# Seven modulation groups moved under the first feed forward, the scan's backward keys into the context attention

## The reference, cut to what matters

```python
s_lat = jax.nn.silu(c)[:, None, :]
s_ctx = jax.nn.silu(c_ctx)[None, None, :]
for i in range(DEPTH):
    need_ctx = i < DEPTH - 1
    ml = jnp.split(s_lat @ w_ada[i] + b_ada[i], 6, axis=-1)
    mc = jnp.split(s_ctx @ w_ada[i] + b_ada[i], 6, axis=-1)
    u_lat = modulate(h_lat, g_pre_mix[i], ml[0], ml[1])
    ...
    h_lat = h_lat + ml[2] * rms_norm_2(o_lat, g_post_mix[i])
    f_lat = sqrelu_mlp(modulate(h_lat, g_pre_ff[i], ml[3], ml[4]), w_ff1[i], w_ff2[i])
    h_lat = h_lat + ml[5] * rms_norm_2(f_lat, g_post_ff[i])
    if need_ctx:
        h_ctx = h_ctx + mc[2] * rms_norm_2(o_ctx, g_post_mix[i])
        ...
```

## Time and profile before

| | |
|---|---|
| median of 3 runs | 1934.95 us (1932.95 to 1937.16) |
| the profiled execution | 1936.78 us, span 1934.9 us |
| granted clock of PE, mean of the span | 0.995 |
| PE busy | 1869.8 us (97%) |
| DVE busy | 1105.8 us (57%) |
| ACT busy | 861.6 us (45%) |
| POOL busy | 211.9 us (11%) |

### The profile page before, as it was taken

The page is one execution under the profiler, slowest core; times in us unless marked ns, Lnnn a source line. Parts: engine busy times, 40 slices in busy tenths (PEclk is TensorE's granted clock), DMA queues, the critical chain, the costliest instruction groups (busy, mean ns, idle before and its releaser), DMA issues. The chain is left out here.

```text
span 1934.9 us, 37112 instructions
## 1 busy us (share of the span) xinstructions
PE 1869.8 (97%) x15824; PEld 1559.3 (81%) x15824; DVE 1105.8 (57%) x1835; ACT 861.6 (45%) x1559; POOL 211.9 (11%) x249
## 2 busy tenths in 40 slices
PE   7999999999999999999999999999999999899998
PEld 5768998776899788756898888888887798579986
DVE  6566774566667554476557665444444565546643
ACT  5465653446656542465322335322222254655532
POOL 2101221110122100103122211000000011000000
PEclk9999999999999999999999999999999999899999
DMA  7777665467766541353000042333332234024653
GB/s 267 250 256 224 189 183 175 166 227 263 223 166 195 175 142 55 115 174 110 26 4 4 4 151 65 104 119 98 100 107 88 66 99 139 25 88 133 194 180 124
DMA packets 219354, 264.68 MB, mean 137 GB/s; under 512 B 14214, under 2 KB 153782, under 8 KB 214711
## 3 DMA queue, kind: packets, MB, share of 16 engines
q1 hardware_dynamic: 218603, 261.49, 42.4%
q10 hardware_dynamic: 588, 0.82, 0.1%
HBM read 261.20 MB, written 1.09 MB: 136 GB/s over the span
## 5 line engine op out<-in xcount | busy, mean ns | idle before, releaser
L404 PE MATMUL acc<-rounded,rounded 128*128 128x512 f32 (+1 forms) x2552 | 875.1, 343 | 9.6 <-DVE rounded L684 4.1
L405 PE MATMUL acc<-rounded,rounded 128*128 128x512 f32 (+1 forms) x2552 | 867.0, 340 | 0.0
L406 PE MATMUL acc<-rounded,rounded 128*128 128x512 f32 (+1 forms) x2552 | 866.8, 340 | 0.0
L388 DVE TENSOR_TENSOR rounded<-arena,rounded 128x2048 fp32r<-128x2048 f32 (+1 forms) x194 | 434.3, 2241 | 285.9 <-ACT rounded L377 285.8
L404 PEld LDWEIGHTS acc<-rounded,rounded 128*128 128x128 f32 x2552 | 480.6, 188 | 80.1 <-issue 14.7
L405 PEld LDWEIGHTS acc<-rounded,rounded 128*128 128x128 f32 x2552 | 480.7, 188 | 60.0 <-issue 1.9
L406 PEld LDWEIGHTS acc<-rounded,rounded 128*128 128x128 f32 x2552 | 480.5, 188 | 60.0
L377 ACT ACTIVATE rounded<-arena 128x2048 fp32r<-128x2048 f32 (+1 forms) x194 | 362.9, 1873 | 341.6 <-PE acc L406 296.4
L1624 DVE SCALAR_TENSOR_TENSOR arena<-acc,pcol,arena 128x254 f32<-128x254 f32 (+1 forms) x176 | 76.8, 478 | 52.3 <-ACT arena L1605 50.8
L2200 PE MATMUL sc<-arena 64*64 64x64 f32 x2560 | 94.7, 221 | 8.8 <-DVE arena L2350 7.7
L2764 ACT ACTIVATE arena<-acc 128x512 f32<-128x512 f32 (+1 forms) x64 | 31.4, 490 | 159.6 <-PE acc L406 159.6
(11 more groups left out here) (265 smaller groups left out, 1691.6 us busy)
## 6 DMA issues: line engine op xcount, KB each, us to landing
arena<-in_w_ff SPq DMA_DIRECT2D x64, 1024.0 KB, 5.4
arena<-in_w_ada SPq DMA_DIRECT2D x48, 1024.0 KB, 5.1
arena<-in_w_up SPq DMA_DIRECT2D x88, 512.0 KB, 5.1
arena<-in_w_in SPq DMA_DIRECT2D x24, 1024.0 KB, 5.3
arena<-in_w_down SPq DMA_DIRECT2D x20, 1024.0 KB, 5.0
arena<-in_w_out SPq DMA_DIRECT2D x16, 1024.0 KB, 5.1
arena<-in_w_in_even SPq DMA_DIRECT2D x9, 1024.0 KB, 5.3
arena<-in_w_in_odd SPq DMA_DIRECT2D x8, 1024.0 KB, 5.2
```

Of the source, the lines that this page charges most:

```text
L388: dve.tensor_tensor(r32(w), w, r32(high_slot(c)[:, 0:size(c)]), ALU.subtract).then_inc(split_made, 1)
L404: pe.matmul(ps, ah, bh, start=first, stop=False)
L405: pe.matmul(ps, ah, bl, start=False, stop=False)
L406: return pe.matmul(ps, al, bh, start=False, stop=last)
```

## The change

- Blocks 16 to 22 leave attBl and attBc; only block 23 is still made in attBl's first two units, and attBc makes none. Each of the seven becomes two "late" chunks in the list, one ahead of ff1(e) and one ahead of the following ff2 (14 chunks). Their first half (4 of 8 row blocks) and second half are summed by DVE, four operations a chunk: 128 x 512 weights times the column of silu(c), into `late_sum`. PE then makes 4 products of `late_sum` with a matrix of ones (`late_pe`), which sum over the partitions and turn the row into columns, at the start of the second column block of ff2(e). DVE adds the bias. Only the latent stream's value is made.
- DVE makes the decays in projB, after the running sums; the keys of direction 0 in attBl's units 0 to 3, those of direction 1 in attBc's units 0 to 3.
- In all attentions by feature POOL copies the two reciprocals to 128 x 128 (`widen`), and PE transposes that in place of the two broadcast products. POOL's eight products of attBc are spread between these copies.
- Gains and gates of layer 1 are made in proj1 (one gain in scan step 0), its gates are transposed, stored and read back there.

The core of the diff (changed call arguments, buffers and bookkeeping of banks are left out):

```diff
@@ -326,6 +326,21 @@
                 partial[0] += 1
                 release.extend([(chunk_read, partial[0]), (sc_full, fill_of(n) + 1)])
 
+        late_read = sem("late_read")
+        late_chunk = []
+
+        def plan_late():
+
+            n = len(late_chunk)
+            view = I["w_ada_2"][1].rearrange("(k p) n -> p k n", p=P)
+            c, k0 = 512 * (4 + n // 2), 4 * (n % 2)
+            late_chunk.append(len(chunks))
+            whole.add(len(chunks))
+            chunks.append(view[:, k0:k0 + 4, c:c + 512])
+            release.append((late_read, n + 1))
+            if n % 2:
+                stage(("late", n // 2), tr=1)
+
         def is_up(g):
             return len(chunks[g].shape) == 4
 
...
@@ -383,6 +398,7 @@
             while splits["low"] < len(split_chunks) and split_chunks[splits["low"]] <= g:
                 n = splits["low"]
                 c = split_chunks[n]
+                late_dve(dve, c)
                 dve.wait_ge(high_made, n + 1)
                 w = raw_slot(c)[:, 0:size(c)]
                 dve.tensor_tensor(r32(w), w, r32(high_slot(c)[:, 0:size(c)]), ALU.subtract).then_inc(split_made, 1)
...
@@ -465,10 +481,9 @@
             stage(("prep", j), sc=2, tr=2)
         stage("kT", tr=4)
         stage("qT", tr=4)
-        stage("attBl", acc=16, tr=16 + 4, sc=8 + 4)
-        plan_ada(range(16, 20), lambda n: sc_at["attBl"] + 3 * n)
-        stage("attBc", acc=16, tr=8 + 4 + 8, sc=8 + 4)
-        plan_ada(range(20, 24), lambda n: sc_at["attBc"] + 3 * n)
+        stage("attBl", acc=16, tr=16 + 1, sc=8 + 1)
+        plan_ada([23], lambda n: sc_at["attBl"])
+        stage("attBc", acc=16, tr=8 + 8, sc=8)
         for s in range(NCH):
             if s == 1:
                 stage("gates", tr=1)
...
@@ -490,10 +505,14 @@
         EIGHTHS, ET = 8, FT2 // 8
 
         def plan_ff1(e):
+            if e:
+                plan_late()
             stage(("ff1", e), acc=ET)
             plan_feat(("ff1", e), I["w_ff1_2"][0][:, e * ET * P:(e + 1) * ET * P], pairs(ET * P), pair_fills(("ff1", e), ET))
 
         def plan_ff2(e):
+            if e < EIGHTHS - 1:
+                plan_late()
             stage(("ff2", e), acc=8)
             plan_tok(("ff2", e), I["w_ff2_2"][0][e * ET * P:(e + 1) * ET * P, :], ET, acc_at[("ff2", e)], [ALL] * 2)
             if e == EIGHTHS - 1:
...
@@ -898,17 +918,16 @@
                     for m in range(2):
                         pe.matmul(ps[m * HD:(m + 1) * HD, 0:P], self.v(u, m, kb), self.probT[:, u % 2, (m * n + kb) * P:(m * n + kb + 1) * P],
                                   start=(kb == 0), stop=(kb == n - 1), tile_position=(0, m * HD))
-                pe.wait_ge(att_comb, self.base + u + 1)
-                for m in range(2):
-                    ins = pe.matmul(ps[m * HD:(m + 1) * HD, P:2 * P], self.recip[:, 2 * u + m:2 * u + m + 1].broadcast_to([P, HD]), ident,
-                                    start=True, stop=True, tile_position=(0, m * HD))
+                i = self.featured.index(u)
+                pe.wait_ge(att_wide, self.spread_units + i + 1)
+                ins = pe.transpose(ps[:, P:2 * P], self.wide[:, i % 2, :], ident)
                 ins.then_inc(POOLS[self.values_at(u)[0]][1], 1)
 
             def tensor(self, pe, hook=None):
                 self.scores(pe, 0)
                 self.scores(pe, 1)
                 for u in range(self.n):
-                    if self.ada:
+                    if u < 2 * len(self.ada):
                         ada_pe(pe, self, u // 2, u % 2)
                     if self.group is not None and u % 2 == 0:
                         group_pe(pe, self.group, u // 2)
...
@@ -993,6 +1010,17 @@
                                             self.recip[:, 2 * u:2 * u + 2].unsqueeze(2).broadcast_to([P, 2, HD]), ALU.mult)
                 ins.then_inc(drain(*f), 1)
 
+            def widen(self, pool, before=None):
+
+                for i, u in enumerate(self.featured):
+                    if before and u in before:
+                        before[u]()
+                    pool.wait_ge(att_comb, self.base + u + 1)
+                    if i >= 2:
+                        pool.wait_ge(att_spread, self.spread_units + i - 1)
+                    pool.tensor_copy(self.wide[:, i % 2, :].rearrange("p (m e) -> p m e", m=2),
+                                     self.recip[:, 2 * u:2 * u + 2].unsqueeze(2).broadcast_to([P, 2, HD])).then_inc(att_wide, 1)
+
             def outputs_by_feature(self, dve, u):
 
                 f = self.values_at(u)
...
@@ -1238,7 +1266,46 @@
-        mod_gates = mod_gate.rearrange("p l w k s -> p (l w k s)")
+        gates_of = [mod_gate[:, l].rearrange("p w k s -> p (w k s)") for l in range(DEPTH)]
+        late_done = [0]
+
+        def late_dve(dve, c):
+
+            while late_done[0] < len(late_chunk) and late_chunk[late_done[0]] + 2 <= c:
+                n = late_done[0]
+                late_done[0] += 1
+                if n and n % 2 == 0:
+                    late_add(dve, n // 2 - 1)
+                g = late_chunk[n]
+                wait_landed(dve, g)
+                if n % 2:
+                    dve.wait_ge(late_read, n)
+                w = shaped(raw_slot(g), g)
+                for k in range(4):
+                    s = silu_c[:, 4 * (n % 2) + k, 0:1]
+                    if n % 2 == 0 and k == 0:
+                        ins = dve.tensor_scalar(late_sum, w[:, k, :], s, None, ALU.mult)
+                    else:
+                        ins = dve.scalar_tensor_tensor(late_sum, w[:, k, :], s, late_sum, ALU.mult, ALU.add)
+                    if k < 3:
+                        link(dve, ins)
+                ins.then_inc(late_read, 1)
+
+        def late_pe(pe, b):
+
+            pe.wait_ge(late_read, 2 * b + 2)
+            ps = claim(pe, "tr", tr_at[("late", b)])
+            for n in range(4):
+                ins = pe.matmul(ps[:, 2 * n:2 * n + 2], late_sum[:, n * P:(n + 1) * P], ones[:, 0:2], start=True, stop=True)
+            ins.then_inc(tr_full, 1)
+
+        def late_add(dve, b):
+
+            f = tr_at[("late", b)]
+            ps = filled(dve, "tr", f)
+            dve.tensor_tensor(mod[:, 1, 16 + 4 * b:20 + 4 * b, :], ps[:, 0:8].rearrange("p (a b) -> p a b", a=4),
+                              col("b_ada_2", 6 * KT + 16 + 4 * b, 4).unsqueeze(2).broadcast_to([P, 4, 2]), ALU.add)\
+               .then_inc(drain("tr", f), 1)
...
@@ -1328,18 +1395,32 @@
+        def pre_gain(dve, l, w):
+
+            scale = mod[:, l, (3 * w + 1) * KT:(3 * w + 2) * KT, :]
+            pre = col(("g_pre_mix_2", "g_pre_ff_2")[w], KT * l, KT).unsqueeze(2).broadcast_to([P, KT, 2])
+            return dve.scalar_tensor_tensor(mod_gain[:, l, w], scale, 1.0, pre, ALU.add, ALU.mult)
+
+        def post_gate(dve, l, w):
+
+            gate = mod[:, l, (3 * w + 2) * KT:(3 * w + 3) * KT, :]
+            post = col(("g_post_mix_2", "g_post_ff_2")[w], KT * l, KT).unsqueeze(2).broadcast_to([P, KT, 2])
+            return dve.tensor_tensor(mod_gate[:, l, w], gate, post, ALU.mult)
+
+        def ada_gains(dve):
+
+            wait_drained(dve, "tr", tr_at[("group_turn", 2)])
+            for w in range(2):
+                pre_gain(dve, 0, w)
+                post_gate(dve, 0, w).then_inc(mod_ready, 1)
+
+        def late_gains(dve):
+
+            wait_drained(dve, "tr", tr_at[("late", EIGHTHS - 2)])
+            wait_drained(dve, "tr", att_bl.ada_tr[0])
+            pre_gain(dve, 1, 1)
+            for w in range(2):
+                post_gate(dve, 1, w).then_inc(mod_ready, 1)
...
@@ -1505,6 +1586,9 @@
+
+        def pool_att1(pool, l):
+            att[("att1", l)].widen(pool, {13: lambda: subnorm_pool(pool, l)})
...
@@ -1730,6 +1816,7 @@
+        late_sum = Region(at_ff0_end + 9 * SEQ).take(512)
...
@@ -1913,6 +2000,8 @@
+            for d in range(2):
+                decays_dve(dve, d)
...
@@ -2017,10 +2106,8 @@
-                if u < 2:
-                    decays_dve(dve, u)
-                else:
-                    kd_dve(dve, *divmod(u - 2, 4))
+                if u < 4:
+                    kd_dve(dve, 0, u)
...
@@ -2064,6 +2151,8 @@
+                if u < 4:
+                    kd_dve(dve, 1, u)
...
@@ -2074,11 +2163,21 @@
-            pool.wait_ge(prep_done, 8)
-            for d in range(2):
-                for j in range(4):
-                    wait_drained(pool, "tr", att.more[3 if d else j])
-                    pool.tensor_tensor(kka[d][:, j, :], kk[:, j, :], rates[d][:, j, :], ALU.mult).then_inc(kka_done, 1)
+            pool.wait_ge(prep_done, 4)
+
+            def key_rates(*pairs):
+
+                def place():
+                    for d, j in pairs:
+                        wait_drained(pool, "tr", att.more[3 if d else j])
+                        if d:
+                            pool.wait_ge(prep_done, 8)
+                        pool.tensor_tensor(kka[d][:, j, :], kk[:, j, :], rates[d][:, j, :], ALU.mult).then_inc(kka_done, 1)
+
+                return place
```

(24 more changed lines are left out.)

61 lines of the change are left out of this document (29 added, 32 removed).

## The result

The changed kernel takes 1926.6 us (median of 1923.64, 1926.61 and 1926.82), the kernel before 1936.06 beside it: a ratio of 0.9944, 95% interval 0.9926 to 0.9962. In a second set on another occasion it was 1927.75 against 1935.48, 0.9958 (0.9946 to 0.9969). So it is faster, by 8 to 11 us. A fourth run of the changed kernel, at a granted clock of 0.757 over the whole span, took 2251 us and is left out as disturbed. The profiled execution took 1926.8 (span 1925.0) against 1936.8 (span 1934.9): 10.0 us less. The second profile of the same kernel has a span of 1924.1.

What follows compares the result with a forecast made beforehand. PE, busy 97% of the span, was taken as the bound. The terms -8.5 - 7 - 5 + 7 = -13.5 us made 1936.8 into 1923.3 for the profiled execution, 1921.5 us for the median, range 1911 to 1935.

Steps and rivals of the forecast that it cites:

- attBl, -8.5: attBl: three of four modulation groups, decays and cheaper broadcasts shorten it by 8.5 us, bounds -5 to -11.
- the 1.3 us put back for missed handovers: attBl: laid out at -9.8 us, taken as -8.5 for some four missed handovers of 0.2 to 0.4 us.
- rival (b): DVE or handovers pace attBl (-5) and attBc (-3), broadcasts bring -2: 1932 us; sign: late attBl PE gaps; chance 0.15.
- attBc, -7: attBc: four modulation groups and cheaper broadcasts leave PE, DVE paces units 0 to 3: 7 us shorter, bounds -3 to -11.
- the 2.7 us put back for the clock and the handovers: attBc: laid out at -9.7 us, 2 us put back for the clock and 0.7 for handovers, giving -7.
- Broadcasts elsewhere, -5: att1, attC and attD: 32 units lose 0.2 us each if PE sets the unit; taken as -5, bounds -6.4 and +1.
- Feed forward, +7: First feed forward: seven sets of late products on PE's path add 7 us (6.4 to 7.4), DVE's added work hidden.
- the margin of 4.0 us: Feed forward: DVE's subtraction for split weights ends 4.0 us before PE wants it, with 2.9 us of modulation ahead; 0 stall expected.
- a slot freed "about 6 us before ACT asks": Feed forward: a modulation chunk's slot is freed about 6 us before ACT asks for the next part; loads take 5.1 us.
- (a): Feed forward: PE waits for split weights; 1.9 us a round cancels the gain, 4 us makes 1949 us; chance 0.13.
- (c): Lower clock spreads over attBc and into the scan: 6 us more, 1928 us; sign: attBc clock under 0.9; chance 0.12.
- (d): PE's whole saving comes through: -11 - 11 - 6.4 + 6.4 = -22, 1913 us; chance 0.10.

Runs made afterwards that it cites:

- x3: Changed kernel with both decays and all eight key steps back in attBl's units, none ahead of the ropes or in attBc: ratio 0.9977 to the kernel before.
- x5: Changed kernel with one small PE product in place of four in each of the seven late sets: ratio 0.9918 to the kernel before.
- x4: Changed kernel with the old broadcasts and the old places of decays and keys, only the seven groups moved: ratio 0.9992 to the kernel before.
- x2: Kernel before with only the broadcasts changed (POOL's copies, one PE transpose), POOL's key products placed between the copies: ratio 0.9981 to the kernel before.
- x11: Changed kernel with key steps spread: three behind the decays, the others in attBl's units, none in attBc: ratio 0.9947 to the kernel before.
- x7: Changed kernel with eight DVE operations in place of four for each of the 14 late chunks: ratio 0.9979 to the kernel before.
- x13: Changed kernel with early scores and maxima at two attention seams, keys spread out of attBc, one late chunk taken one weight part later: ratio 0.9967.
- x9: Changed kernel with dummy PE products where PE would wait in attBl, attBc, attC and attD: ratio 0.9960 to the kernel before.

## Why the prediction was right, and where it was not

The time and the order of the parts came out as forecast; one term was more than twice too large, and two of the stage lengths agree in part by luck.

**attBl, -8.5: measured -8.4 and -8.6.** The maxima of unit 4 start 15.6 us after the stage (848.76 after 833.15), laid out by hand at 15.7. The reason that the layout gave is not what the rows show: the prediction had DVE pacing units 0 to 3, but from 837.0 to 849.3 PE has no gap, and DVE waits 1.10 us for it in between:
```profile
843.23 0.29 DVE L1031 COPY arena<-sc 128x128 f32<-128x128 f32 x1 [1.10 <-PE sc L923]
```
The group that stays, block 23, costs PE 2.9 us just there, and the prediction's PE unit of 3.1 left it out; so PE and DVE are about level. x3 shows that DVE takes over at once when the decays and keys come back. From unit 4's maxima on the stage took 18.3 us, laid out at 16.8; the 1.3 us put back for missed handovers covered that. PE's gaps in the last units (0.85 to 0.98) end with ACT, and not with DVE or POOL, which the prediction had named as its sign of rival (b).

**attBc, -7: measured -8.0 and -7.9.** DVE paces the first units, at 4.1 us, not 3.8 (the minimum that ends with POOL's product in each, 0.67 us in place of 0.16, is 0.5 of it); unit 4's maxima come 14.6 us after the start, laid out at 14.4, and the rest took 14.8 us against 13.3. So the bare layout (-9.7) was 1.7 too good, and the 2.7 us put back for the clock and the handovers 1.0 too many. What the 1.5 us of the second half are was not taken apart. The lower clock came, 0.88 over the stage in both profiles, under the 0.9 that the prediction had called a sign of being wrong; but it fell where DVE is the longer one. No run shows the 2 us put back for the clock, which were the author's estimate: the rows showed a dip that cost nothing up to 17.5 us into the stage (29.4 and 29.5 us) and 1.1 us at 18 to 22 (x5, 30.6).

**Broadcasts elsewhere, -5: this is the step that was mis-sized.** 0.13 for the transpose was 0.17, and the products ahead of it take 0.1 longer: 0.11 a unit in place of 0.2. 32 units give at most 3.5. The two att1 show up to 0.3 us each. attC with attD is 1.4 and 3.0 us shorter in the two profiles, but that is the clock as well: x4, which has the old broadcasts, takes 63.4 us there, less than the changed kernel's 64.0. Profiles at about the same clock differ by 1.0 (x2 against the kernel before, 0.93 and 0.94) and 1.3 (x11 against x4, both 0.97). That makes about 2 in place of 5, as rival (b) had it for this part, and 3 of the 5 us between 1921.5 and the measured 1926.6; another 1.1 is that the kernel before took 1936.06 beside it and not 1934.95. That it is the sequence (products on half the columns, then a full transpose) that makes the products 0.1 longer is read from rows alone; no run changed it by itself.

**Feed forward, +7: measured +7.7.** Seven sets made 6.2 (6.4 expected from the 0.92 in a row), no weight part was late, and the margin of 4.0 us held against 2.9 more in x7. What was missed is a consumer that the prediction had not listed behind DVE: the near bias, 1.4 us with what follows. The question it put, what is queued behind the waiting or added instruction on its engine, was asked for the split weights only. The other margin, a slot freed "about 6 us before ACT asks", was not there: ACT waits for loads in 17 copies. That this costs nothing rests on PE being further behind ACT, which the prediction had not worked out.

**Rivals.** (a) did not come, but x13 shows that its chain is real and near: 3.1 us for one late slot. (b) is out for the attentions: their units shrank. (c) came as a clock and not as time in the two profiles of the changed kernel; in x5 and x7 a dip later in the same stage cost 1.1 us, so it is a matter of a microsecond and of the place. (d) is out.

The sum over the profiled execution, part by part: -1.3 ahead of the first att1, -0.3 to the second att1, +2.1 from there to attBl (403.2 us against 401.1; the other profile has 400.8, and over the second att1 the granted clock is 0.95 here and 1.00 there), -16.4 in attBl and attBc, +7.5 from there to attC, -1.4 in attC and attD, -0.1 behind them: -9.9 us of span. The first and third of these are of stages that the change leaves nearly alone, and they are what two executions of one kernel differ by.

## What to carry to other kernels

Work taken off the busiest engine pays only as far as the next engine is cleared too: seven groups moved alone gave nothing measurable, and with the small edits that relieved DVE and PE's units the change gave 8 us. An idle gap on an engine is room only for what stands ahead of the wait; behind it, the same instruction lengthens the chain (x11: a key behind a wait of 1.94 us made the next maxima start 1.4 us later). When work is added to an engine, list every consumer behind it, not only the one that feeds the busiest loop, and for a shared ring of slots ask when the added reader frees its slot. A stage's length in one profile holds the place of a clock dip as well (29.4 to 30.7 us for the same instructions of attBc): compare several profiles of the same code before a microsecond is given to an edit.

## What was not expected of the hardware

In attD of the changed kernel the fp32 transpose of 128x128 behind products on 64 columns took 0.17 us from its start to the next one (1687.51 to 1687.68), and the products ahead of it 1.02 (from 1686.49); ahead of the two broadcast products of the kernel before they took 0.93 (1695.81 to 1696.74). In x7, behind a wait of 4.05 us, the granted clock was 0.50 from 1458 to 1463 and the products of 128x512 started 0.43 us apart in place of 0.23; in the changed kernel, behind a wait of 1.15 us at the same place, the clock was 1.00 from 1455 to 1460. In attBc every profile of the changed kernel's code had the clock at 0.50 for 3.4 or 6.8 us, at different places, and x9, whose gaps were filled, had it too (from 882 to 886); where this lay up to 17.5 us into the stage, attBc took 29.4 or 29.5 us, with such a stretch at 18 to 22 us 30.6 (x5) and 30.7 (x7).
